# A chunked state-space scan on TensorE: held and moving operands exchanged, two heads in the column halves, outputs turned back and gated a step later

## Chip, cores and metric

One core of one Trainium2 chip runs the whole program, a two-block transformer stack in fp32, in one launch. The metric is the device time in microseconds (us) from start to end of an execution, as the median of several.

## What is computed

The first block holds a Mamba-2 branch beside differential attention; the rest (three feed-forward layers, projections, a second attention block) is not touched. The part that matters, cut down:

```python
SSD_HEADS, SSD_GROUPS, SSD_HEAD_DIM, SSD_STATE, SSD_CHUNK = 32, 4, 64, 128, 128     # 256 tokens: 2 chunks
X = x * dt                                        # (b, nc, Q, G, E, P), E = 8 heads of a group
a_cum = jnp.cumsum(dt * a_head, axis=-1)
Lmat = jnp.exp(jnp.where(causal, a_cum[..., :, None] - a_cum[..., None, :], -jnp.inf))
CB = jnp.einsum('bclgn,bcsgn->bgcls', Cc, Bc)
y_diag = jnp.einsum('bgcls,bgecls,bcsgep->bclgep', CB, Lmat, X)
states = jnp.einsum('bclgn,bgecl,bclgep->bcgepn', Bc, jnp.exp(a_cum[..., -1:] - a_cum), X)
y_off = jnp.einsum('bclgn,bcgepn,bgecl->bclgep', Cc, prev, jnp.exp(a_cum))
y = y_diag + y_off + d_skip * x
y = rmsnorm(group of (y * silu(z))) * norm_g      # groups of 512 channels
return y @ w_branch
```

## The kernel before

Every weight is cut into units of 1 MB that pass through a ring of five slots. SyncE loads a unit into RAW when TensorE has used the unit five before it (`w_used`); ScalarE rounds it to the high part WH (`split_hi`, L494); VectorE subtracts to get the low part WL (`split_lo`, L1092); TensorE then multiplies high by high, high by low and low by high (`parts`, L1803 to L1805). These two splits go on in every stage, one pair per unit.

There is no planner: each engine has its own block of code, executed in the order in which it is written, and the engines meet in named semaphores. The scan has eight blocks n = 2g + c (group g, chunk c) and nine steps r = 0 to 8. Step r prepares block r and multiplies block r-1, and between the steps stand one or two of the weight units of the q, k, v and gate projections (`beside(r)`: two in steps 2, 4, 6, 8).

- GpSimd (L1020 to L1044): `spread_cum(r + 1)` fetches the cumulated decay of the next block, spread over all partitions, into one of two DECAY buffers (L1029), after the products of block r-1 have been made (`ssd_y`). Then the skip term of block r goes to Y (L1042), which waits until block r-1 is normalised (`ys_ok`), as Y has one buffer.
- ScalarE (L777 to L801): eight Relu, one per head, and an Exp over 128x1024 turn the fetched rows into the decay matrices of block r (L784, L787). Then the state of a c = 0 block is copied (L792), and of the gated block r-1 the sum of squares and the reciprocal root are taken (L795, `rsqrt`). Then the weight splits and copies of the units beside.
- VectorE (L1410 to L1451): X dt of block r (L1418, which waits for `ssd_y`, as XDT has one buffer), for c = 0 also XDEC (L1420); block r-1: add the products from PS[3] (L1427), for c = 1 scale and add the part from the state (L1430, L1432), gate with silu(z) (L1434, signals `y_gated`); the masked CB (L1437), decay times CB (L1441, signals `ssd_m`); block r-1 normalised (L1444); the splits.
- TensorE (L2093 to L2129): CB of block r (L2099), for block r-1 the state product (L2111 or L2114) into PS[6], then eight products, one per head: the masked decay block 128x128 is held, XDT of 64 columns moves, and the output (tokens x 64) goes to PS[3] (L2117). fp32 operands make two passes each. Then the units beside.

```python
ins = mm(PS[3][:, e * SSD_P:(e + 1) * SSD_P], DECAY[n % 2][:, e, :], XDT[:, e * SSD_P:(e + 1) * SSD_P],
         start=True, stop=True)
```

In step 8 TensorE runs both gate units and turns the first normalised rows (`turn_rows`, L1987, into PS[7]); ScalarE and VectorE make high and low parts of them (L625, L1257), and the first gate sums are copied out (L761, `gate0_kept`). Then come the eight attention heads: scores (L2148, L2149), masked by VectorE (L1468), exponentials (L816), normalising (up to L1488, signals `attn_ok`), the transposes of the probabilities (L2141). Between them stand the units of ssd_w_branch, which multiply the turned scan outputs.

The rows of the second block's attention at L2306 (`pair_values`) also serve below: there two heads write to the two partition halves of PS[6], with a held operand 64 wide.

## Time and profile before

| | |
|---|---|
| median of 3 runs | 1108.06 us (1108.05 to 1108.44) |
| the profiled execution | 1108.8 us, span 1107.2 us |
| mean granted TensorE clock | 0.998 |
| TensorE busy | 1096.7 us, 99% of the span |
| VectorE busy | 770.8 us, 70% |
| ScalarE busy | 619.2 us, 56% |
| GpSimd busy | 36.5 us, 3% |
| DMA | 202.27 MB, mean 183 GB/s |

The span runs from the first to the last instruction of the profiled execution; the run's own time lies 1.6 us above it. Busy shares are means over the whole program. A busy TensorE need not be at its peak, since ends of matmuls are modelled; the start times are what tells a standstill. The scan occupies about 328 to 420 us.

### The profile page before, as it was taken

The numbers are of one execution on the slowest core, as the hardware profiler recorded it, in microseconds if no ns is written. First come the engines' busy times: TensorE is split into PE (matmuls) and PEld (weight loads), VectorE is DVE, ScalarE is ACT, GpSimd is POOL, SyncE is SP. The second block draws the span as 40 slices with busy tenths as digits, with TensorE's granted clock in tenths as the row PEclk, the third lists the DMA queues.
The fourth block names the chain that finished last, engine by engine and source line by source line (L and its number), as shares of the span: only waits on it lengthen the run. The fifth ranks groups of instructions, "written<-read, shape, count | busy, mean of one in ns | idle before, by whom it ended". The sixth has DMA issues, their size and how long they took to land.

```text
span 1107.2 us, 14788 instructions
## 1 busy us (share of the span) xinstructions
PE 1096.7 (99%) x6046; PEld 935.7 (85%) x6046; DVE 770.8 (70%) x897; ACT 619.2 (56%) x883; POOL 36.5 (3%) x66
## 2 busy tenths in 40 slices
PE   9999999999999999999999999999999999999997
PEld 7888888899999987778878888888978778888886
DVE  5866766687767778868768666675785667666664
ACT  7544445564577766655455454456776636444443
POOL 0000000000001100000000000000021100000000
PEclk9999999999999999999999999999999999999999
DMA  9656654755666545345566655645643445555551
GB/s 331 237 190 190 190 191 157 233 180 184 190 190 192 183 143 208 127 155 193 167 208 197 192 188 190 191 151 181 206 139 131 171 152 191 191 189 190 190 190 39
DMA packets 131667, 202.27 MB, mean 183 GB/s; under 512 B 5088, under 2 KB 98144, under 8 KB 131344
## 3 DMA queue, kind: packets, MB, share of 16 engines
q1 hardware_dynamic: 127920, 189.82, 52.7%
q0 software_dynamic: 2672, 10.65, 2.8%
q8 instruction: 48, 0.79, 0.3%
q10 hardware_dynamic: 1008, 0.86, 0.2%
q14 instruction: 19, 0.16, 0.0%
HBM read 200.24 MB, written 1.08 MB: 182 GB/s over the span
## 4 chain that ended last, share of the span: by engine, by line
PE 92%; DVE 3%; ACT 2%; issue 1%; DMA 1%; SPq 0%; DVEq 0%; ACTq 0%
PE TOP L1874 20%; PE ACC L1803 14%; PE ACC L1805 13%; PE ACC L1804 13%; PE TOP L1877 10%; PE TOP L1803 4%; PE TOP L1805 4%; PE TOP L1804 4%; ACT WH L494 1%; DVE WL L1092 1%; PE ACC L2117 1%; PE TOP L1719 1%; DMA H<-in_x 1%; PE TOP L2306 1%; PE TOP L2291 1%
## 5 line engine op out<-in xcount | busy, mean ns | idle before, releaser
L1092 DVE TENSOR_TENSOR WL<-RAW,WH 128x2048 fp32r<-128x2048 f32 (+3 forms) x177 | 400.1, 2264 | 114.0 <-ACT WH L494 113.7
L494 ACT ACTIVATE WH<-RAW 128x2048 fp32r<-128x2048 f32 (+1 forms) x179 | 337.6, 1890 | 68.7 <-DMA RAW<-in_ffn_w_gate 29.6
L1874 PE MATMUL TOP<-XT,WH 128*128 128x512 f32 x960 | 239.9, 392 | 0.0
L1874 PEld LDWEIGHTS TOP<-XT,WH 128*128 128x128 f32 x960 | 174.3, 189 | 32.4
L1803 PE MATMUL ACC<-WH,KTH 128*128 128x512 f32 (+1 forms) x452 | 178.6, 395 | 0.0
L1804 PE MATMUL ACC<-WL,KTH 128*128 128x512 f32 (+1 forms) x452 | 175.6, 389 | 0.0
L1805 PE MATMUL ACC<-WH,KTL 128*128 128x512 f32 (+1 forms) x452 | 175.6, 388 | 0.0
L1877 PEld LDWEIGHTS TOP<-XT,WL 128*128 128x128 f32 x960 | 131.0, 190 | 9.4
L1877 PE MATMUL TOP<-XT,WL 128*128 128x256 f32 x960 | 133.9, 282 | 0.0
L540 ACT ACTIVATE SCR<-TOP 128x512 f32<-128x512 f32 x60 | 35.8, 596 | 162.0 <-PE TOP L1877 162.0
L1805 PEld LDWEIGHTS ACC<-WH,KTL 128*128 128x128 f32 x452 | 84.8, 188 | 17.9
L1803 PEld LDWEIGHTS ACC<-WH,KTH 128*128 128x128 f32 x452 | 85.0, 188 | 17.1 <-DVE KTL L1259 0.7
L1804 PEld LDWEIGHTS ACC<-WL,KTH 128*128 128x128 f32 x452 | 85.1, 188 | 15.4
L1136 DVE TENSOR_TENSOR SCR<-TOP,SCR 128x512 f32<-128x512 f32 x60 | 41.4, 691 | 74.4 <-ACT SCR L540 74.4
L1803 PE MATMUL TOP<-WH,XT 128*128 128x512 f32 (+1 forms) x184 | 73.3, 398 | 0.4 <-DVE WL L1092 0.2
L1805 PE MATMUL TOP<-WH,XT 128*128 128x512 f32 (+1 forms) x184 | 71.2, 387 | 0.0
L1804 PE MATMUL TOP<-WL,XT 128*128 128x512 f32 (+1 forms) x184 | 71.1, 387 | 0.0
L1803 PE MATMUL ACC<-XT,WH 128*128 128x256 f32 x208 | 59.3, 285 | 0.0
L1804 PE MATMUL ACC<-XT,WH 128*128 128x256 f32 x208 | 58.8, 283 | 0.0
L1805 PE MATMUL ACC<-XT,WL 128*128 128x256 f32 x208 | 58.8, 283 | 0.0
L1803 PE MATMUL ACC<-WH,XT 128*128 128x512 f32 x144 | 58.4, 405 | 0.1
L1805 PE MATMUL ACC<-WH,XT 128*128 128x512 f32 x144 | 56.4, 391 | 0.0
(311 smaller groups left out, 1452.1 us busy)
## 6 DMA issues: line engine op xcount, KB each, us to landing
RAW<-in_w_in SPq DMA_DIRECT2D x50, 1024.0 KB, 5.2
RAW<-in_ffn_w_down SPq DMA_DIRECT2D x22, 1024.0 KB, 5.0
RAW<-in_ffn_w_gate SPq DMA_DIRECT2D x20, 1024.0 KB, 5.3
RAW<-in_ffn_w_up SPq DMA_DIRECT2D x20, 1024.0 KB, 5.4
RAW<-in_w_down SPq DMA_DIRECT2D x11, 1024.0 KB, 4.9
RAW<-in_w_gate SPq DMA_DIRECT2D x10, 1024.0 KB, 5.3
RAW<-in_w_up SPq DMA_DIRECT2D x10, 1024.0 KB, 5.3
RAW<-in_ssd_w_branch SPq DMA_DIRECT2D x8, 1024.0 KB, 5.0
```

The source lines that it names most:

```text
L494: nc.scalar.activation(WH[:, s, 0:n], RAW[:, s, 0:n], ACT.Copy).then_inc(w_hi, 1)
L540: nc.scalar.activation(LOW[n], TOP[:, bank:bank + 2, TOK:2 * TOK], ACT.Copy).then_inc(low_kept, 1)
L1092: tt(WL[:, s, 0:n], RAW[:, s, 0:n], WH[:, s, 0:n].bitcast(F32), ALU.subtract).then_inc(w_lo, 1)
L1136: tt(by_block(dst), TOP[:, bank:bank + 2, 0:TOK], LOW[n], ALU.add).then_inc((gate_sum, up_sum)[n], 1)
L1719: ins = nc.tensor.transpose(PS[6 + q][:, k * P:(k + 1) * P], XN[:, t, j * P:(j + 1) * P], IDENT)
L1803: mm(ps, stat_hi, mov_hi, start=first, stop=False)
L1804: mm(ps, stat_hi, mov_lo, start=False, stop=False)
L1805: return mm(ps, stat_lo, mov_hi, start=False, stop=last)
L1874: mm(PS[bank], WH[:, slot(c), ws], XT[:, k, :, :].rearrange("p u t -> p (u t)"), start=k == 0, stop=False)
L1877: ins = mm(PS[bank][:, TOK:2 * TOK], WL[:, slot(c), ws], XTH[:, k, :], start=False, stop=k == KD - 1)
L2117: ins = mm(PS[3][:, e * SSD_P:(e + 1) * SSD_P], DECAY[n % 2][:, e, :], XDT[:, e * SSD_P:(e + 1) * SSD_P], start=True, stop=True)
L2291: ins = nc.tensor.transpose(PS[5][:, b * P:(b + 1) * P], SC[q % 2][:, b * P:(b + 1) * P], IDENT)
```

## The change

The products of a block are made the other way round: XDT of a head (128 x 64) is held, the masked decay block of 128 columns moves, and the output is (64 channels x 128 tokens). Even heads go to partitions 0 to 63 of PS[7], odd heads to 64 to 127, so they use the two column halves of the array. The output is thus turned. ScalarE copies it to a free part of V or GAIN (`heads_turned`, signals `yt_kept`), and in the next step TensorE turns it back into PS[3] with four transposes (`turn_back`, signals `y_turned`). VectorE adds, gates and normalises block r-2 in step r (`gated`, `normed`), ScalarE takes its squares there (`squares`, with the discarded output in PS[3] instead of T1, as T1 now holds the scaled state part for a step, `off_ok`). The last block is turned back, gated and normalised among the gate units of step 8. Since PS[7] is taken, the second v unit moves to banks 4 and 5, and the first gate unit to banks 0 and 1, with their waits. GpSimd's code is the same.

```diff
--- before.py
+++ after.py
@@ -318,6 +318,7 @@
             sem, ("dt_abs", "dt_exp", "a_ok", "cums", "cums_exp", "cum_columns"))
         ssd_cb, ssd_cbm, ssd_e, ssd_m, xdec_ok, ssd_y, ssd_st = map(
             sem, ("ssd_cb", "ssd_cb_masked", "ssd_decay", "ssd_mix", "ssd_xdec", "ssd_y", "ssd_state"))
+        yt_kept, y_turned, off_ok = map(sem, ("y_turned_kept", "y_turned_back", "off_diagonal_scaled"))
         state_ok, skip_ok, y_read, y_gated, y_rms, ys_ok = map(
             sem, ("state_ok", "skip_ok", "y_read", "y_gated", "y_rms", "ys_ok"))
         k_turned, k_hi, k_lo = map(sem, ("k_turned", "k_hi", "k_lo"))
@@ -363,7 +364,7 @@
             return U_GATE + 2 * n - 2 if n else U_GATE0
 
         def gate_bank(n, t):
-            return ((4, 0), (4, 5), (6, 7), (4, 5))[n][t]
+            return ((0, 1), (4, 5), (6, 7), (4, 5))[n][t]
 
         def in2_bank(n, t):
             return ((4, 5), (0, 1), (4, 5))[n][t]
@@ -375,7 +376,11 @@
             return 5 - n % 2 if n else 0
 
         def v_bank(n, t):
-            return ((0, 1), (7, 5))[n][t]
+            return ((0, 1), (4, 5))[n][t]
+
+        def heads_turned(n):
+
+            return V[:, 0, 0:512] if n < 4 else GAIN[:, 0:512]
 
 
         def slot(c):
@@ -772,6 +777,12 @@
                         nc.scalar.activation(V[:, t, (n - 9) * 256:(n - 7) * 256], PS[v_bank(n // 2 - 4, t)][:],
                                              ACT.Copy).then_inc(qkv_kept, 1)
 
+            def squares(n):
+
+                act.wait_ge(y_gated, n + 1)
+                own.inc(nc.scalar.activation(PS[3][:], Y, ACT.Square, accum_out=SS[:, 4:5]))
+                rsqrt(RS[:, 4:5], SS[:, 4:5], n + 1, y_rms, 1.0 / GW)
+
             qkv(U_QKV)
             u = U_QKV + 1
             for r in range(9):
@@ -787,16 +798,17 @@
                     nc.scalar.activation(E, E, ACT.Exp, scale=-1.0).then_inc(ssd_e, 1)
                 if r:
                     n = r - 1
+                    act.wait_ge(ssd_y, r)
+                    nc.scalar.activation(heads_turned(n), PS[7][:], ACT.Copy).then_inc(yt_kept, 1)
                     if n % 2 == 0:
                         act.wait_ge(ssd_st, n + 1)
                         nc.scalar.activation(STATE, PS[6][:], ACT.Copy).then_inc(state_ok, 1)
-                    act.wait_ge(y_gated, n + 1)
-                    act.wait_ge(ssd_m, min(r + 1, 8)) if r < 8 else None
-                    own.inc(nc.scalar.activation(T1, Y, ACT.Square, accum_out=SS[:, 4:5]))
-                    rsqrt(RS[:, 4:5], SS[:, 4:5], n + 1, y_rms, 1.0 / GW)
+                if r >= 2:
+                    squares(r - 2)
                 for _u in range(beside(r)):
                     if u == U_GATE0 + 1:
                         kt_hi(0, 0)
+                        squares(7)
                     qkv(u)
                     u += 1
 
@@ -1406,6 +1418,22 @@
             def heads_bc(ap):
                 return ap.unsqueeze(2).to_broadcast([P, HPG, SSD_P])
 
+            def gated(n):
+
+                g, c = divmod(n, 2)
+                dve.wait_ge(skip_ok, n + 1)
+                dve.wait_ge(y_turned, n + 1)
+                own.link(tt(Y, PS[3][:], Y, ALU.add))
+                if c:
+                    own.link(tt(Y, Y, T1, ALU.add))
+                tt(Y, Y, BUF2[:, c, g * GW:(g + 1) * GW], ALU.mult).then_inc(y_gated, 1)
+
+            def normed(n):
+
+                g, c = divmod(n, 2)
+                dve.wait_ge(y_rms, n + 1)
+                stt(BUF2[:, c, g * GW:(g + 1) * GW], Y, RS[:, 4:5], GAIN[:, g * GW:(g + 1) * GW], ALU.mult, ALU.mult).then_inc(ys_ok, 1)
+
             split_lo()
             for r in range(9):
                 if r < 8:
@@ -1419,19 +1447,14 @@
                     if c == 0:
                         tt(by_head(XDEC), by_head(XDT), heads_bc(EX[:, 1, c, g * HPG:(g + 1) * HPG]),
                            ALU.mult).then_inc(xdec_ok, 1)
-                if r:
-                    n = r - 1
-                    g, c = divmod(n, 2)
-                    dve.wait_ge(skip_ok, r)
-                    dve.wait_ge(ssd_y, r)
-                    own.link(tt(Y, PS[3][:], Y, ALU.add))
-                    if c:
-                        dve.wait_ge(ssd_st, r)
-                        own.link(tt(by_head(T1), by_head(PS[6][:]),
-                                    heads_bc(EX[:, 0, c, g * HPG:(g + 1) * HPG]), ALU.mult))
-                        own.link(tt(Y, Y, T1, ALU.add))
-                    zs = BUF2[:, c, g * GW:(g + 1) * GW]
-                    tt(Y, Y, zs, ALU.mult).then_inc(y_gated, 1)
+                if r >= 2:
+                    gated(r - 2)
+                if r and r % 2 == 0:
+
+                    g, c = divmod(r - 1, 2)
+                    dve.wait_ge(ssd_st, r)
+                    tt(by_head(T1), by_head(PS[6][:]), heads_bc(EX[:, 0, c, g * HPG:(g + 1) * HPG]),
+                       ALU.mult).then_inc(off_ok, 1)
                 if r < 8:
                     dve.wait_ge(ssd_cb, r + 1)
                     tt(CBM[:], PS[2][:, 0:P], UPTO, ALU.mult).then_inc(ssd_cbm, 1)
@@ -1439,16 +1462,15 @@
                     dve.wait_ge(ssd_e, r + 1)
                     E = DECAY[r % 2]
                     tt(E, E, CBM[:].unsqueeze(1).to_broadcast([P, HPG, P]), ALU.mult).then_inc(ssd_m, 1)
-                if r:
-                    dve.wait_ge(y_rms, r)
-                    stt(zs, Y, RS[:, 4:5], GAIN[:, g0(n) * GW:(g0(n) + 1) * GW], ALU.mult, ALU.mult).then_inc(ys_ok, 1)
-                else:
-                    def g0(n):
-                        return n // 2
+                if r >= 2:
+                    normed(r - 2)
                 for _u in range(beside(r)):
                     if r == 8 and _u:
                         kt_lo(0)
+                        dve.wait_ge(off_ok, 4)
+                        gated(7)
                     split_lo()
+            normed(7)
 
 
             slopes = [2.0 ** (-8.0 * (h + 1) / DA_HEADS) for h in range(DA_HEADS)]
@@ -2082,9 +2104,18 @@
                     channels(u, q_bank(n))
                 elif n % 2 == 0:
                     v = n // 2 - 4
-                    first_half(u, (v_bank(v, 0), v_bank(v, 1)), lambda t: pe.wait_ge(qkv_kept, 7) if v else pe.wait_ge(conv_done, 12))
+                    first_half(u, (v_bank(v, 0), v_bank(v, 1)), lambda t: pe.wait_ge(qkv_kept, 7 + v) if v else pe.wait_ge(conv_done, 12))
                 else:
                     second_half(u, (v_bank(n // 2 - 4, 0), v_bank(n // 2 - 4, 1)))
+
+            def turn_back(n):
+
+                pe.wait_ge(yt_kept, n + 1)
+                if n:
+                    pe.wait_ge(y_rms, n)
+                for b in range(4):
+                    ins = nc.tensor.transpose(PS[3][:, b * P:(b + 1) * P], heads_turned(n)[:, b * P:(b + 1) * P], IDENT)
+                ins.then_inc(y_turned, 1)
 
             qkv(U_QKV)
             pe.wait_ge(conv_silu, 12)
@@ -2103,31 +2134,34 @@
                     g, c = divmod(n, 2)
 
                     if n:
-                        pe.wait_ge(y_gated, n)
+                        turn_back(n - 1)
                     pe.wait_ge(cums_exp, 1)
                     pe.wait_ge(cum_cols, 1)
                     if c == 0:
                         pe.wait_ge(xdec_ok, n // 2 + 1)
+                        if n:
+                            pe.wait_ge(off_ok, n // 2)
                         mm(PS[6][:], B0[:, g * P:(g + 1) * P], XDEC, start=True, stop=True).then_inc(ssd_st, 1)
                     else:
                         pe.wait_ge(state_ok, n // 2 + 1)
                         mm(PS[6][:], CT[:, g, P:TOK], STATE, start=True, stop=True).then_inc(ssd_st, 1)
                     pe.wait_ge(ssd_m, r)
+
                     for e in range(HPG):
-                        ins = mm(PS[3][:, e * SSD_P:(e + 1) * SSD_P], DECAY[n % 2][:, e, :], XDT[:, e * SSD_P:(e + 1) * SSD_P],
-                                 start=True, stop=True)
+                        ins = mm(PS[7][(e % 2) * SSD_P:(e % 2 + 1) * SSD_P, (e // 2) * P:(e // 2 + 1) * P],
+                                 XDT[:, e * SSD_P:(e + 1) * SSD_P], DECAY[n % 2][:, e, :], start=True, stop=True)
                     ins.then_inc(ssd_y, 1)
                 for _u in range(beside(r)):
                     if u < U_GATE0:
                         qkv(u)
                     elif u == U_GATE0:
-                        first_half(u, (4, 0), lambda t: pe.wait_ge(qkv_kept, 8 + t))
+                        first_half(u, (0, 1), lambda t: pe.wait_ge(qkv_kept, 9 + t))
                         pe.wait_ge(qkv_kept, 12)
+                        turn_back(7)
                         turn_rows(0, BUF2, 0)
                     else:
-                        second_half(u, (4, 0))
+                        second_half(u, (0, 1))
                     u += 1
-            pe.wait_ge(gate0_kept, 1)
             for h in range(9):
                 if h == 8:
                     pe.wait_ge(s_ready, 8)
```

How the order moves, at two places. TensorE, step 7 (block 6); TOP holds banks 4 to 7 and ACC banks 0 to 3. Before:

```order
L2099 MATMUL ACC<-XN 128x128 [waits ssd_cb_masked]
L2111 MATMUL TOP<-SCAN,SCR 128x512 [waits cum_columns,ssd_xdec,cums_exp,y_gated]
L2117 MATMUL ACC<-SCAN,SCR 128x64 [waits ssd_mix]
L2117 MATMUL ACC<-SCAN,SCR 128x64 x7
```

Now:

```order
L2130 MATMUL ACC<-XN 128x128 [waits ssd_cb_masked]
L2117 MATMUL ACC<-TAB,GAIN 128x128 [waits y_rms,y_turned_kept]
L2117 MATMUL ACC<-TAB,GAIN 128x128 x3
L2144 MATMUL TOP<-SCAN,SCR 128x512 [waits ssd_xdec,off_diagonal_scaled,cum_columns,cums_exp]
L2151 MATMUL TOP<-SCR,SCAN 64x128 [waits ssd_mix]
L2151 MATMUL TOP<-SCR,SCAN 64x128 x7
```

Four transposes stand ahead of the state product, and the moving operand has 128 columns.

VectorE from the first gating operation of step 8 to the first attention head. L1092 is a weight split, L1257 the low part of the turned rows. Before:

```order
L1427 TENSOR_TENSOR SCAN<-ACC,SCAN 128x512 [waits ssd_y,skip_ok]
L1430 TENSOR_TENSOR SCR<-TOP,EX 128x512 [waits ssd_state,dve_steps]
L1432 TENSOR_TENSOR SCAN<-SCAN,SCR 128x512 [waits dve_steps]
L1434 TENSOR_TENSOR SCAN<-SCAN,BUF 128x512 [waits dve_steps]
L1444 SCALAR_TENSOR_TENSOR BUF<-SCAN,RS,GAIN 128x512 [waits y_rms]
L1092 TENSOR_TENSOR WL<-RAW,WH 128x2048 [waits weights_hi]
L1257 TENSOR_TENSOR KTL<-TOP,KTH 128x512 [waits k_hi]
L1092 TENSOR_TENSOR WL<-RAW,WH 128x2048 [waits weights_hi]
L1468 SCALAR_TENSOR_TENSOR SCR<-TAB,TOP 128x384 [waits scores,ys_ok]
```

Now (L1104 is the split, L1269 the low part, L1426 to L1429 `gated`, L1435 `normed`, L1456 the scaled state part):

```order
L1426 TENSOR_TENSOR SCAN<-ACC,SCAN 128x512 [waits y_turned_back,skip_ok]
L1429 TENSOR_TENSOR SCAN<-SCAN,BUF 128x512 [waits dve_steps]
L1456 TENSOR_TENSOR SCR<-TOP,EX 128x512 [waits ssd_state]
L1435 SCALAR_TENSOR_TENSOR BUF<-SCAN,RS,GAIN 128x512 [waits y_rms]
L1104 TENSOR_TENSOR WL<-RAW,WH 128x2048 [waits weights_hi]
L1269 TENSOR_TENSOR KTL<-TOP,KTH 128x512 [waits k_hi]
L1426 TENSOR_TENSOR SCAN<-ACC,SCAN 128x512 [waits y_turned_back,skip_ok,off_diagonal_scaled]
L1428 TENSOR_TENSOR SCAN<-SCAN,SCR 128x512 [waits dve_steps]
L1429 TENSOR_TENSOR SCAN<-SCAN,BUF 128x512 [waits dve_steps]
L1104 TENSOR_TENSOR WL<-RAW,WH 128x2048 [waits weights_hi]
L1435 SCALAR_TENSOR_TENSOR BUF<-SCAN,RS,GAIN 128x512 [waits y_rms]
L1490 SCALAR_TENSOR_TENSOR SCR<-TAB,TOP 128x384 [waits scores,ys_ok]
```

The gating of block 7 (ending in L1429) now stands behind the low part L1269, and a weight split stands between it and its normalisation.

## Rows read from the trace of the kernel before

**Rows 1.** Waits of TensorE's matmuls, 318 to 430 us: total, times, longest
```profile
PE TOP L2141 <- DVE SCR L1488: 0.6, 1, 0.6
```
**Rows 2.** Timeline of TensorE: start us, duration us, engine, line, operation
```profile
426.45 0.39 PE L1805 MATMUL ACC<-WH,KTL 128*128 128x512 f32 x1
427.41 0.55 PE L2141 MATMUL TOP<-TAB,SCR 128*128 128x128 f32 x3 [0.57 <-DVE SCR L1488]
```
**Rows 3.** Chain of waits, 376 to 428 us: start us, us, what
```profile
376.44 1.74 PE ACC L2117 x16
378.21 0.70 DVE SCAN L1418
```
**Rows 4.** Timeline of TensorE, scan products of steps 2 and 4
```profile
338.92 1.89 PE L2117 MATMUL ACC<-SCAN,SCR 128*128 128x64 f32 x16
340.62 0.36 PE L1803 MATMUL TOP<-XT,WH 128*128 128x256 f32 x1
...
361.91 1.89 PE L2117 MATMUL ACC<-SCAN,SCR 128*128 128x64 f32 x16
```
**Rows 5.** Timeline of TensorE, two heads in column halves in the second block
```profile
865.17 0.39 PE L1805 MATMUL ACC<-WH,XT 128*128 128x512 f32 x1
865.49 0.43 PE L2306 MATMUL TOP<-BUF,V 128*64 128x256 f32 x1
...
865.97 0.27 PE L2306 MATMUL TOP<-BUF,V 128*64 128x128 f32 x1
865.98 0.27 PE L2306 MATMUL TOP<-GAIN,V 128*64 128x128 f32 x1
...
866.09 0.27 PE L2306 MATMUL TOP<-GAIN,V 128*64 128x128 f32 x1
866.29 0.44 PE L2291 MATMUL TOP<-TAB,BUF 128*128 128x128 f32 x2
```
**Rows 6.** Timeline of TensorE, four transposes between gate products
```profile
413.82 0.60 PE L1987 MATMUL TOP<-TAB,BUF 128*128 128x128 f32 x4
...
414.48 0.40 PE L1804 MATMUL TOP<-WL,XT 128*128 128x512 f32 x1
```
**Rows 7.** GpSimd: timeline, issues by size with median us to landing, all of L1029
```profile
386.82 0.58 POOL L1029 DMA_DIRECT2D SCR<-cum_rows  x1 [1.81 <-PE ACC L2117]
...
406.95 1.05 POOL L1042 TENSOR_TENSOR SCAN<-BUF,ROWS 128x512 f32<-128x512 f32 x1 [10.80 <-DVE BUF L1444]
...
SCR<-cum_rows POOLq DMA_DIRECT2D x6, 512.0 KB, 4.0
...
DMA to landing us min/median/max: 3.7/4.2/5.0
```
**Rows 8.** Timeline of ScalarE, step 7
```profile
398.85 2.44 ACT L784 ACTIVATE SCR<-SCR,DT 128x128 f32<-128x128 f32 x8
...
402.28 0.58 ACT L792 ACTIVATE SCAN<-TOP 128x512 f32<-128x512 f32 x1
404.89 0.63 ACT L795 ACTIVATE SCR<-SCAN 128x512 f32<-128x512 f32 x1 [2.03 <-DVE SCR L1441]
...
406.11 1.91 ACT L494 ACTIVATE WH<-RAW 128x2048 fp32r<-128x2048 f32 x1
```
**Rows 9.** Timeline of VectorE, steps 7 and 8 to the first head
```profile
401.92 0.69 DVE L1427 TENSOR_TENSOR SCAN<-ACC,SCAN 128x512 f32<-128x512 f32 x1
...
403.57 1.22 DVE L1441 TENSOR_TENSOR SCR<-SCR,CBM 128x1024 f32<-128x1024 f32 x1
406.12 0.75 DVE L1444 SCALAR_TENSOR_TENSOR BUF<-SCAN,RS,GAIN 128x512 f32<-128x512 f32 x1 [1.32 <-ACT RS L500]
408.06 2.29 DVE L1092 TENSOR_TENSOR WL<-RAW,WH 128x2048 fp32r<-128x2048 f32 x1 [1.19 <-ACT WH L494]
410.26 0.68 DVE L1427 TENSOR_TENSOR SCAN<-ACC,SCAN 128x512 f32<-128x512 f32 x1
...
421.34 1.01 DVE L1468 SCALAR_TENSOR_TENSOR SCR<-TAB,TOP 128x384 f32<-128x384 f32 x2
```

## The prediction

> **What bounds the kernel now.** The page first: a mean granted clock of 0.998 (2.4 GHz), and TensorE busy in 99% of the span, so the first question is whether the scan costs TensorE time. The list of waits over 318 to 430 us then says that TensorE is held there by another engine once, before the transposes of the first attention head, by VectorE [rows 1]. In order of time this is a gap of 0.96 us between two matmul starts [rows 2] where 0.23 is usual, so 0.73 us of real standstill. The reader is to see that this one gap decides what a saving in the scan is worth. The chain of waits says what leads to it: after the scan matmuls that start at 376.44 it leaves TensorE and stays with VectorE and ScalarE until 427.41 [rows 2, 3]. TensorE can gain whatever it likes between these times; the first head's transposes move only if the vector and scalar chain moves. Behind them TensorE is full again, so **the time of the kernel moves by as much as that start moves**.
>
> **TensorE's work.** I number scan steps by the loop index r; step r holds the products of block r-1. Old products: 16 passes (eight heads, two passes each), from first start to the next matmul 1.70 us [rows 4]. The new form (stationary operand 64 wide, 128 moving columns, two heads in the two column halves) exists in the second block's attention: both halves start 0.00 to 0.01 us apart, and the 128-column passes follow each other at 0.11 us [rows 5]. Four head pairs of two passes are 8 x 0.11 = 0.88 us. Entering costs 0.32 instead of 0.23 us (865.17 to 865.49), leaving 0.20 instead of 0.11 (866.09 to 866.29): 0.09 + 0.09. So 1.06 us, and 0.64 less per step, 5.1 for eight. The outputs now have to be turned back: four transposes per block. From 413.82 to 414.48 there are four of them and one 0.23 us matmul [rows 6]: 0.43 us, eight times 3.5 us. Net TensorE saves 0.21 us per step and 1.6 us before the first head.
>
> The row shows what a switch into and out of column halves costs, 0.18 us together. The Trainium skill, "TensorEngine Tiling (Array Packing)", Overview, promises up to 2x where a free dimension is at most 64, and says under Key Properties that changing the tiling mode drains the engine. By its 2x alone the eight steps would cost 6.8 instead of 13.6 us and TensorE would save 3.3 us in all; the trace agrees with the drain, and the sum goes by the rows.
>
> **The copy out on ScalarE** (PS[7] to V or GAIN) is one 128x512 copy per step as for STATE, 0.58 us of which some 0.1 overlaps what follows, so 0.48 [rows 8]; it lies before the squares. VectorE's operations are the same ones, moved. The squares now write to PS[3], for which no row stands: between 0.05 us less and 0.1 us more each; I take nothing. Moving v and gate banks adds no wait that I find, since the copies that free them are a unit old.
>
> **The queue that nothing was changed in: GpSimd.** Its order is: fetch decay block r+1, multiply the skip term of block r (which waits for the normalised block r-1, ys_ok), fetch block r+2, and so on. Before, the normalisation of block r-1 stood in step r, and the fetch waited for the scan matmuls alone (1.81 us idle before it) [rows 7]. Now block r-2 is normalised in step r, after that step's mask multiply, and the next fetch stands behind the skip multiply that waits for it. So a loop closes: fetch, ScalarE's eight Relu and Exp 3.43, copies 0.48 (0.96 in every second step), squares to reciprocal root 1.22 [rows 8], 0.83 from the start of the normalisation to that of the skip [rows 7, 9], skip 1.05, fetch 4.0 from issue to landing [rows 7]. That is 11.0 and 11.5 in turn, just over 11.2 us a step. Two steps take TensorE 22.99 us now (338.92 to 361.91 [rows 4]), less 2 x 0.21: 11.3 us each. The loop just fits, with almost nothing to spare.
>
> **The walk to the first head,** in the time of the profiled run. The scan of step 5 is released at 376.44 now [rows 3]; four steps have saved 0.21 each by then: 375.6, done 1.0 later. VectorE: X dt 0.7 [rows 3]; add, gate and CB mask 1.65, one more add for this block 0.72; decay multiply 1.23 [rows 9]: the normalisation of block 3 starts at 380.9. Skip 381.8, fetch 382.8, landed 386.8. ScalarE 3.43 + 0.48 + 1.22: 391.9. Skip, fetch, landed 0.83 + 1.05 + 4.0 later: 397.8. ScalarE with two copies: 403.4, block 5 normalised. Then the tail, where VectorE's and ScalarE's splits (2.20 and 1.91 us [rows 8, 9]) alternate with it: ScalarE split and VectorE split 407.5, gating of block 6 1.33, squares 1.22: 410.1 (block 6 is normalised at 406.12 now). Two splits again: 414.2. Low part of the turned rows 0.6 (a 128x512 operation that nothing waits for at once), gating of block 7 three times 0.72: 417.0. Squares: 418.2. ScalarE split 420.2, VectorE split 422.4, last normalisation: 423.2. The first head's scores are masked at 421.34 now [rows 9]. **The first head comes 1.8 us later**, although TensorE would be there 1.6 us earlier. What costs this: the gating of block 7, which starts at 410.26 [rows 9], now stands behind a weight split of each engine and the low part of the turned rows, and starts at 414.9; one weight split less follows it. TensorE will show two waits: up to 2 us for the copies of the first gate sums, which now stand behind these squares and a split on ScalarE (done at 420.2 + 1.0), and 2 to 3 us before the first head.
>
> The profiled run took 1108.8 us, the median of the runs shown is 1108.06, 0.7 below. Against the median: 1108.06 + 1.8 = **1109.9 us**. A measurement of this kernel can tell about 0.2%, 2.2 us, from no change; the forecast is on the slow side of none.
>
> **Rivals.**
> 1. *The fetch loop binds harder.* The median over the scan is 4.0 us; all eight fetches lie between 3.7 and 5.0 [rows 7], and they will now start at other moments of the weight loads. If they take 4.6, each of the four rounds from step 4 on adds 0.6 or nearly: 2.4 us, 1112.3; with another 0.3 us per round for GpSimd's order 1113.5. For: 11.2 against 11.3 leaves no slack. Against: the median of six in this very stretch is 4.0. It decides from a round above 11.3 us. Chance 0.22.
> 2. *The halves don't overlap here.* Passes of the two halves one after the other: 16 x 0.11 + 0.18 = 1.94 us, and TensorE loses 0.24 + 0.43 a step, 5.4 us, 1113 to 1116. Against: [rows 5] are the same form, source kind and bank sharing. Chance 0.05.
> 3. *TensorE leads the chain after all.* If the reorder takes the gating off VectorE's path and the fetches land in 3.7 us, the chain follows the earlier ends of the scan, and the 1.6 us are paid out: 1106.5. For: in the chain of before, ends of the scan release VectorE [rows 3]. Against: the gating of block 7 starts 4.6 us later, as walked. Chance 0.07.
> 4. *The halves are worth their full factor* and TensorE leads: 1108.06 - 3.3 = 1104.8, faster by 0.3%. In rows this is a block of 0.85 us with nothing to enter or leave, against the 0.18 measured. It is what the 2x of the page cited above would do. Chance 0.05.
>
> **How the numbers follow.** The forecast, 1108.6 to 1111.2 for its own terms (0.3 us per fetch either way over two to four rounds), has 0.61. Rival 1 reaches to 1113.5. The range from 1107.6 to 1113.3 leaves out rivals 3 and 4, nearly all of 2 and the end of 1. Slower by over 0.2% (above 1110.3) is rival 1, rival 2 and a quarter of the forecast, 0.42; faster by over 0.2% (under 1105.8) is rival 4, 0.05; the rest, 0.53, is within 0.2%.
>
> **What the changed profile would show.** The scan block of TensorE at about 1.06 us from first start to the next matmul, the halves starting together; four transposes in 0.43 us. ScalarE's first Relu of a step idle for the cum_rows transfer, up to 4 us in the steps after a short one (r = 4, 6) and about 1 us in r = 5 and 7. GpSimd's skip ahead of each fetch, which starts within 0.1 us of its end. VectorE's split of weights waiting some 3 us for ScalarE in the tail, TensorE waiting for gate0_kept and 2 to 3 us before the first head. Wrong would be: no wait of ScalarE for cum_rows (then the loop isn't there and the tail alone stands), a TensorE wait inside the scan (then the loop is slower than I walk it), or the first head's masked scores less than 46 us after the scan of step 5 starts (44.9 now, 47.6 as walked).

## The result, and the profile after

The changed kernel takes 1116.43 us (median of six runs, 1113.43 to 1118.12) against 1108.06 us for the kernel before (1107.94 to 1108.44): a ratio of 1.0072, 95% interval 1.0062 to 1.0082. It is slower by 8.4 us. The forecast was 1109.9 with a range to 1113.3, so the sign of its lean was right and its size was not. The profiled run of the change is the slowest of its six, 1.7 us above their median.

| | before | after |
|---|---|---|
| median of the runs, us | 1108.06 | 1116.43 |
| lowest to highest, us | 1107.94 to 1108.44 | 1113.43 to 1118.12 |
| profiled run: time, span, mean granted clock | 1108.8, 1107.2, 0.998 | 1118.12, 1116.1, 0.994 |
| first head's transposes start, us | 427.41 | 435.91 |

The first weight load of the stretch is issued at 323.08 us before and at 323.17 after, so the two traces can be laid side by side. The start of the first head's transposes moved by 8.5 us and the span by 8.9, so the bookkeeping of the prediction (the kernel's time moves by as much as that start) comes out to 0.4 us. Two things that it doesn't hold nearly cancel in this. Behind that start the granted clock of the change is 0.5 from 436.96 for 3.4 us, and the last weight load is issued at 1082.76 us against 1072.93, 9.8 us later. From there to the end of the span it is 33.4 us, against 34.3 before; why is not shown. The loss in the span arises between 323 and 441 us.

First what came as forecast. TensorE's timeline, step 5 (start us, duration us, engine, line, operation):

```profile
374.39 0.60 PE L2117 MATMUL ACC<-TAB,V 128*128 128x128 f32 x4
374.82 1.02 PE L2144 MATMUL TOP<-SCAN,SCR 128*128 128x512 f32 x2
375.78 1.09 PE L2151 MATMUL TOP<-SCR,SCAN 128*64 128x128 f32 x16
376.80 0.50 PE L1825 MATMUL ACC<-WH,XT 128*128 128x512 f32 x1
```

The turning back takes 0.43 us (374.39 to 374.82), and the sixteen passes 1.02 us (375.78 to 376.80) where they took 1.70 [rows 4]. So the two column halves do overlap. Now the waits, 318 to 440 us (engine, line, what it waited for: total us, times, longest):

```profile
POOL SCAN L1054 <- DVE BUF L1435: 76.4, 7, 13.2
...
ACT SCR L795 <- DMA SCR<-cum_rows: 16.8, 5, 6.1
...
DVE SCR L1464 <- ACT SCR L798: 8.3, 4, 4.5
...
PE ACC L2117 <- ACT RS L505: 3.5, 1, 3.5
```

ScalarE waits 16.8 us for the fetched decay blocks, VectorE's mask multiply 8.3 us behind it, and TensorE, inside the scan, once, 3.5 us, for a reciprocal root. GpSimd's timeline shows why. A DMA_DIRECT2D row is a fetch, TENSOR_TENSOR the skip multiply, and the brackets are the idle time before it:

```profile
345.48 1.03 POOL L1054 TENSOR_TENSOR SCAN<-BUF,ROWS 128x512 f32<-128x512 f32 x1 [13.19 <-DVE BUF L1435]
346.46 0.58 POOL L1041 DMA_DIRECT2D SCR<-cum_rows  x1
360.08 1.03 POOL L1054 TENSOR_TENSOR SCAN<-BUF,ROWS 128x512 f32<-128x512 f32 x1 [13.04 <-DVE BUF L1435]
361.07 0.59 POOL L1041 DMA_DIRECT2D SCR<-cum_rows  x1
...
374.84 0.58 POOL L1041 DMA_DIRECT2D SCR<-cum_rows  x1
...
388.25 0.59 POOL L1041 DMA_DIRECT2D SCR<-cum_rows  x1
...
399.27 0.57 POOL L1041 DMA_DIRECT2D SCR<-cum_rows  x1
```

Each fetch starts at the end of a skip multiply, as forecast. Most of them don't land as forecast. The view of the fetch lines over 318 to 440 us, and SyncE's timeline of the weight loads:

```profile
DMA to landing us min/median/max: 4.0/5.8/7.1
```
```profile
345.85 0.37 SPq L400 DMA_DIRECT2D RAW<-in_w_in  x1
360.10 0.37 SPq L400 DMA_DIRECT2D RAW<-in_w_in  x1
374.36 0.37 SPq L400 DMA_DIRECT2D RAW<-in_w_in  x1
```

The median of six was 4.0 before [rows 7] and is 5.8 now. The fetches at 346.46, 361.07 and 374.84 start 0.61, 0.97 and 0.48 us behind a weight load of 1 MB and take 7.1, 6.8 and 5.9 us. The one at 388.25, with no load within 5 us ahead of it, takes 4.0. Before, a fetch stood some 3.1 us behind its load (361.02 and 364.10). The DMA view of 345.8 to 349.9 us, by queue, tells what the fetch does in that time (packets, MB, share; q1 is SyncE's queue, q0 GpSimd's, and a queue without packets has no line):

```profile
q1 hardware_dynamic: 436, 0.89, 70.7%
```

In the 3.4 us after its issue the fetch has not one packet; the load has all 436. Some of this is there without a load too: the fetch issued at 388.25 has no packet before 389.5 either. But from 347.8 to 349.9 the load alone fills the 16 engines to 98.3% of their time (first line below), and only with the load's last packets do those of the fetch begin, 349.9 to 350.5 (the other two lines):

```profile
q1 hardware_dynamic: 381, 0.78, 98.3%
```
```profile
q1 hardware_dynamic: 90, 0.16, 67.8%
q0 software_dynamic: 28, 0.11, 46.4%
```

Both queues run on the same 16 engines (GpSimd's fills 100% of them from 390 to 391 us), and the fetch **waits until the weight load has nearly drained**, some 2 us more than it needs without a load. The distance alone doesn't fix the time: in experiment 8 a fetch stands 0.61 us behind its load as well and lands after 5.8 us, not 7.1.

What follows from the late fetch is a standstill of TensorE inside the scan. Timeline of ScalarE, then of TensorE:

```profile
380.80 2.45 ACT L795 ACTIVATE SCR<-SCR,DT 128x128 f32<-128x128 f32 x8 [3.11 <-DMA SCR<-cum_rows]
...
385.20 0.60 ACT L783 ACTIVATE ACC<-SCAN 128x512 f32<-128x512 f32 x1
```
```profile
382.56 0.49 PE L2130 MATMUL ACC<-XN 128*128 128x128 f32 x2
386.53 1.08 PE L2117 MATMUL ACC<-TAB,GAIN 128*128 128x128 f32 x4 [3.48 <-ACT RS L505]
```

The transposes of block 4 wait for the reciprocal root of block 3 (the bank PS[3]). Its squares stand on ScalarE's queue behind eight Relus that wait for a fetch. The products themselves could not have started before 385.7 in any case, since VectorE's mask multiply waits for the same Relus and ends there (384.44, 1.23 us long); the wait for the root puts the transposes and the state product behind this as well. What that share costs was not tested. And the 3.48 us aren't all that is lost. The table of stretches (core 0: us, PE busy, PEld, DVE, ACT, POOL, then PEclk, DMA share, GB/s):

```profile
383.00:386.00 3.00, 0.05 (x1) 0.00 (x0) 1.23 (x1) 2.94 (x7) 0.00 (x0) 0.96 0.73 217
386.00:389.00 3.00, 2.47 (x6) 1.25 (x6) 1.39 (x2) 2.27 (x3) 1.58 (x2) 0.50 0.36 138
389.00:392.00 3.00, 3.00 (x19) 2.33 (x19) 2.35 (x2) 0.00 (x0) 0.00 (x0) 0.50 0.55 175
392.00:395.00 3.00, 3.00 (x13) 2.38 (x13) 2.78 (x5) 2.67 (x9) 0.00 (x0) 0.90 0.00 0
```

TensorE stood still, and the granted clock then was 0.50 (1.2 GHz) from 385.8 to 392.6 us; products that start 0.23 us apart start 0.43 us apart there. Last the tail, VectorE and TensorE:

```profile
421.52 0.68 DVE L1426 TENSOR_TENSOR SCAN<-ACC,SCAN 128x512 f32<-128x512 f32 x1
...
426.86 2.29 DVE L1104 TENSOR_TENSOR WL<-RAW,WH 128x2048 fp32r<-128x2048 f32 x1 [3.21 <-ACT WH L499]
429.07 0.74 DVE L1435 SCALAR_TENSOR_TENSOR BUF<-SCAN,RS,GAIN 128x512 f32<-128x512 f32 x1
429.84 1.02 DVE L1490 SCALAR_TENSOR_TENSOR SCR<-TAB,TOP 128x384 f32<-128x384 f32 x2
```
```profile
435.91 0.55 PE L2175 MATMUL TOP<-TAB,SCR 128*128 128x128 f32 x3 [2.14 <-DVE SCR L1510]
```

The masks of the first head start at 429.84 (421.34 in [rows 9]), with VectorE's split waiting 3.21 us for ScalarE's and TensorE 2.14 us before the head, behind which the granted clock falls to 0.5 once more. The tail has the shape that was walked, 6.6 us later than walked.

### The profile page after: what moved, and what is told of

The parts are those of the page before. It is cut to its first block, busy times and chain, and to the rows that moved or that the text cites. A ratio compares the mean times of both kernels' runs of the same rounds, so it can differ in the third digit from the quotient of the medians.

```text
span 1116.1 us, 14853 instructions
## 1 busy us (share of the span) xinstructions
PE 1100.3 (99%) x6078; PEld 934.4 (84%) x6078; DVE 770.9 (69%) x897; ACT 623.5 (56%) x891; POOL 36.2 (3%) x66
## 4 chain that ended last, share of the span: by engine, by line
PE 87%; ACT 4%; DMA 4%; DVE 3%; issue 1%; POOL 0%; ACTq 0%; DVEq 0%
PE TOP L1896 20%; PE ACC L1825 13%; PE ACC L1827 13%; PE ACC L1826 13%; PE TOP L1899 10%; PE TOP L1825 3%; PE TOP L1827 3%; PE TOP L1826 3%; DMA SCR<-cum_rows 3%; ACT SCR L795 1%; ACT WH L499 1%; PE TOP L1741 1%; DMA RAW<-in_ffn_w_up 1%; PE TOP L2340 1%; PE TOP L2325 1%
## 5 line engine op out<-in xcount | busy, mean ns | idle before, releaser
L1104 DVE TENSOR_TENSOR WL<-RAW,WH 128x2048 fp32r<-128x2048 f32 (+3 forms) x177 | 400.3, 2266 | 114.6 <-ACT WH L499 114.3
L1825 PE MATMUL TOP<-WH,XT 128*128 128x512 f32 (+1 forms) x176 | 69.9, 397 | 1.2 <-DVE WL L1310 0.9
L1827 PE MATMUL TOP<-WH,XT 128*128 128x512 f32 (+1 forms) x176 | 68.1, 387 | 0.0
L1826 PE MATMUL TOP<-WL,XT 128*128 128x512 f32 (+1 forms) x176 | 68.0, 386 | 0.0
L1825 PE MATMUL ACC<-WH,XT 128*128 128x512 f32 x152 | 62.0, 408 | 0.1
L1827 PE MATMUL ACC<-WH,XT 128*128 128x512 f32 x152 | 59.7, 393 | 0.0
L1826 PE MATMUL ACC<-WL,XT 128*128 128x512 f32 x152 | 59.5, 391 | 0.0
L1825 PE MATMUL ACC<-XT,WH 128*128 128x256 f32 x208 | 59.3, 285 | 0.0
```

The lines of the kernel that those rows point to most:

```text
L1104: tt(WL[:, s, 0:n], RAW[:, s, 0:n], WH[:, s, 0:n].bitcast(F32), ALU.subtract).then_inc(w_lo, 1)
L1825: mm(ps, stat_hi, mov_hi, start=first, stop=False)
L1826: mm(ps, stat_hi, mov_lo, start=False, stop=False)
L1827: return mm(ps, stat_lo, mov_hi, start=False, stop=last)
```

## The experiments

Lines of experiments are those of their own kernels, shifted by one to three from the change's. Each batch had runs of the kernel before beside it: medians of 1108.15 (first four), 1108.08 (next three) and 1108.47 (last three).

**1. The fetch ahead of the skip.** The change, with GpSimd's queue reordered:

```diff
                 if r == 0:
                     spread_cum(0)
-                if r < 7:
-                    spread_cum(r + 1)
+                    spread_cum(1)
+                if r < 6:
+                    spread_cum(r + 2)
```

> The changed kernel, with GpSimd's fetch of decay block r+2 put ahead of skip(r) instead of behind it, so that it waits for scan product r alone. Theory A (queue order): the 8.4 us come from the fetch, which now stands behind a normalisation one step late, starts within 1 us of a 1 MB weight load and lands after 5.6 to 7.1 us instead of 4; each step then waits for it, ScalarE blocks the squares, TensorE stalls 3.75 us and its clock falls to 1.2 GHz. Then here the landings are 4.0 to 4.7 us, the 3.75 us gap and the half clock near 386 us are gone, and the time is 1107.5 to 1110 us. Theory B (the turn-back path itself, products to copy to transposes to gating, costs): no more than 2 us come back, 1114 us or more. Theory C (the new tail ahead of the first attention head costs): the stalls in the scan go, but 1110 to 1113 us stay.

1109.78 us (1108.72 to 1111.04), ratio 1.0015 (1.0006 to 1.0025). In its profile, GpSimd's timeline and the view of the fetch lines, 353 to 385 us:

```profile
353.69 0.57 POOL L1041 DMA_DIRECT2D SCR<-cum_rows  x1 [7.92 <-PE TOP L2152]
...
384.66 0.58 POOL L1041 DMA_DIRECT2D SCR<-cum_rows  x1 [2.37 <-PE TOP L2152]
```
```profile
DMA to landing us min/median/max: 3.8/4.1/4.8
```

The fetch is released by the scan products again, ScalarE waits for none, and TensorE has no gap over 0.9 us before 419 us. (Over 318 to 440 us the six landings lie between 3.8 and 5.4 us; the 5.4 is the first one, 5.6 in the change.) The mean clock is 1.000 in the profiled run and 0.997 to 1.000 in all ten. 6.7 of the 8.4 us are back: theory A. What is left is 1.6 us; the time is within A's range and 0.2 us short of C's. These 1.6 us lie in the tail (experiment 5).

**2. The queue order alone, in the kernel before.** No halves, no turning back, gating unmoved:

```diff
                 if r == 0:
                     spread_cum(0)
-                if r < 7:
-                    spread_cum(r + 1)
+                    spread_cum(1)
...
                                         skip.unsqueeze(2).to_broadcast([P, HPG, SSD_P]), ALU.mult).then_inc(skip_ok, 1)
+                if 1 <= r < 7:
+                    spread_cum(r + 1)
```

> The kernel before, with one edit: GpSimd's fetch of decay block k is queued behind skip(k-1), so that it waits for the normalisation of block k-2 in the step before its use, the same wait that the changed kernel has; no column halves, nothing turned back, gating not moved. Theory A (queue order): this alone costs most of the loss, 1112 to 1118 us, with landings above 5 us where the fetch starts within 1.5 us of a weight load, and 4 us elsewhere. Theory B (the turn-back path costs): close to the kernel before, 1108 to 1109.5 us.

1116.83 us (1116.17 to 1118.07), ratio 1.0077 (1.0060 to 1.0094). A kernel that computes exactly as before is as slow as the change once its fetch stands behind a late normalisation. Theory A, but not the same loop: the fetches follow each other at 12.1 to 14.2 us (353.02, 367.19, 379.26, 392.48), and each round here also holds the mask multiply of 1.22 us, since ScalarE's squares wait for it in the kernel before. Their landings have a median of 4.9 us. The fetches at 367.19 and 392.48, with no load within 6 us ahead, land after 4.0 and 4.1 us, and their rounds are still 12.1 us: here part of the loss is the loop by itself. TensorE stood 1.79 and 1.87 us in two steps, and behind the second the granted clock was 0.5 for 6.8 us, so this one edit brings the clock's part of the loss, too.

**3. Collisions taken away, the loop kept.** The change, with SyncE holding five weight loads:

```diff
                 if c >= RING:
                     sp.wait_ge(w_used, c - RING + 1)
+                k = {8: 3, 10: 4, 11: 5, 13: 6, 15: 7}.get(c - U_QKV)
+                if k:
+                    sp.wait_ge(cum_spread[k % 2], 16 * (k // 2 + 1))
```

> The changed kernel, queue order of GpSimd kept, but SP holds the weight loads that coincide with a fetch (five of them) until that fetch has landed. Theory A1 (the loop fits, as forecast, as long as the fetch lands in 4 us; the weight load ahead of it in the DMA engines is what breaks it): landings 4.0 to 4.6 us, no stall above 1 us in the scan, 1109 to 1111 us. Theory A2 (the loop over GpSimd binds by itself, contention adds little): landings as short, but ScalarE still waits over 1 us per step for them and the time stays 1112 us or more.

1110.85 us (1109.39 to 1112.17), ratio 1.0023 (1.0013 to 1.0034). GpSimd's timeline, and the view of the fetch lines:

```profile
359.42 0.59 POOL L1044 DMA_DIRECT2D SCR<-cum_rows  x1
...
370.93 0.58 POOL L1044 DMA_DIRECT2D SCR<-cum_rows  x1
...
382.37 0.59 POOL L1044 DMA_DIRECT2D SCR<-cum_rows  x1
...
393.03 0.58 POOL L1044 DMA_DIRECT2D SCR<-cum_rows  x1
```
```profile
DMA to landing us min/median/max: 3.7/4.1/5.4
```

With the fetch landing in 4.1 us the rounds are 11.5, 11.4 and 10.7 us, where 11.2 was worked out, and the kernel runs within 1 us of the forecast. (The round before these, from 345.62 to 359.42, takes 13.8 us here as well.) ScalarE still waits for four of the fetches, 9.6 us in all, and VectorE's mask multiply 4.5 us behind it, which was put down as a sign of A2; but TensorE doesn't wait in the scan, and the time is A1's: the loop is as forecast, the landing in the change isn't.

**4. Column halves undone, fetch ahead.** On top of experiment 1, blocks in whole rows into two banks in turn, which the gating and the squares use directly; no copy and no turning back:

```diff
                     for e in range(HPG):
-                        ins = mm(PS[7][(e % 2) * SSD_P:(e % 2 + 1) * SSD_P, (e // 2) * P:(e // 2 + 1) * P],
-                                 XDT[:, e * SSD_P:(e + 1) * SSD_P], DECAY[n % 2][:, e, :], start=True, stop=True)
+                        ins = mm(PS[3 if n % 2 else 7][:, e * SSD_P:(e + 1) * SSD_P], DECAY[n % 2][:, e, :],
+                                 XDT[:, e * SSD_P:(e + 1) * SSD_P], start=True, stop=True)
```

> The changed kernel with the fetch ahead of the skip, and the column halves undone: decay blocks held and inputs moving as before, products straight into one of two banks in turn (no copy to SBUF, no transposes), gating still one step later. The halves save 0.64 us of products and cost 0.43 us of transposes per step, 1.6 us before the first head; so 1 to 2 us more than e1_fetch_ahead if TensorE leads there, no difference (within 0.5 us) if the tail behind the last block sets the start of the first head, and less than e1_fetch_ahead if the copy and the transposes lie on the path to the last gating.

1111.39 us (1110.80 to 1112.72), ratio 1.0033 (1.0019 to 1.0046): 1.6 us more than experiment 1, as eight steps of 0.21 us would give. The copy and the transposes aren't on the path. The expectation tied such a loss to TensorE leading, and it does not lead here: it waits 2.13 us before the first head (2.14 in experiment 1). The tail sets that start in both kernels, but by the traces the tail itself hangs on the products of the scan (VectorE waits 9.4 us for them over the stretch in experiment 1), which come later by those 0.21 us a step.

**5. The last block's squares and normalisation moved out of the tail.** On top of experiment 1:

```diff
                     if u == U_GATE0 + 1:
                         kt_hi(0, 0)
-                        squares(7)
                     qkv(u)
                     u += 1
+            squares(7)
...
                     split_lo()
-            normed(7)
...
-            dve.wait_ge(ys_ok, 8)
+            dve.wait_ge(ys_ok, 7)
...
                     if h:
                         split_lo()
+                    else:
+                        normed(7)
```

(The squares of block 7 also write to T1 there, since PS[3] is taken by then.)

> e1_fetch_ahead with the last block's squares moved on ScalarE behind the two copies of the first gate, and its normalisation on VectorE behind the first head's maxima (into the time in which ScalarE takes the exponentials). Theory (the tail sets the rest): in e1_fetch_ahead the first head's scores are there at 418.8 us and are masked at 422.1, because the weight split waits for the squares (1.2 us) and the normalisation stands before the masks (0.75 us); with both out of the way the masks start near 419 us and the transposes of the first head 2.5 to 3.3 us earlier than in e1_fetch_ahead, so 1106 to 1107.5 us, faster than the kernel before. Rival (TensorE takes over: 424.6 us is as early as it can be at the first head's transposes, or the waits move into the second head): under 1 us of gain, 1109 us or more.

1105.79 us (1105.54 to 1106.63), ratio 0.9976 (0.9967 to 0.9985): 4.0 us under experiment 1, a little more than was expected, and **faster than the kernel before**, by 0.2%. In the profiled runs the first head's transposes start 3.5 us earlier (424.72 for 428.20); four of the ten runs of experiment 1 had a mean clock of 0.997 and took 1110.0 to 1111.0 us, where its profiled one had 1.000 and 1109.0, which may be the rest. VectorE's tail in experiment 1, then in this one, and this one's first head on TensorE:

```profile
415.25 0.69 DVE L1430 TENSOR_TENSOR SCAN<-SCAN,BUF 128x512 f32<-128x512 f32 x1
419.15 2.29 DVE L1105 TENSOR_TENSOR WL<-RAW,WH 128x2048 fp32r<-128x2048 f32 x1 [3.20 <-ACT WH L499]
421.36 0.74 DVE L1436 SCALAR_TENSOR_TENSOR BUF<-SCAN,RS,GAIN 128x512 f32<-128x512 f32 x1
422.13 1.02 DVE L1491 SCALAR_TENSOR_TENSOR SCR<-TAB,TOP 128x384 f32<-128x384 f32 x2
```
```profile
414.90 0.69 DVE L1430 TENSOR_TENSOR SCAN<-SCAN,BUF 128x512 f32<-128x512 f32 x1
415.51 2.28 DVE L1105 TENSOR_TENSOR WL<-RAW,WH 128x2048 fp32r<-128x2048 f32 x1
418.66 1.02 DVE L1490 SCALAR_TENSOR_TENSOR SCR<-TAB,TOP 128x384 f32<-128x384 f32 x2 [0.86 <-PE TOP L2185]
```
```profile
424.20 0.39 PE L1829 MATMUL ACC<-WH,KTL 128*128 128x512 f32 x1
424.72 0.55 PE L2177 MATMUL TOP<-TAB,SCR 128*128 128x128 f32 x3
```

The weight split follows the gating at once, the masks wait for TensorE's scores and for nothing else, and TensorE reaches the first head without the gap.

**6. The same tail in the kernel before.** The same two moves.

> The kernel before, with the same two moves of the last block's squares and normalisation. TensorE finishes the second half of the gate unit at 419.85 us there and the masks start at 421.34, so at most 1 us can be had: 1107 to 1108.1 us. If e5_tail_later gains over e1_fetch_ahead and this one hardly over the kernel before, the changed kernel's TensorE time is worth something only with its tail shortened.

1108.15 us (1107.33 to 1108.42), ratio 0.9999 (0.9990 to 1.0008): nothing. The moves alone are worth nothing to the kernel before; the gain of experiment 5 needs the rest of the change (experiment 10 tells how much of it is the halves').

**7. The deferral undone, halves kept.** The gating, squares and normalisation of block r-1 back in step r, and

```diff
                     ins.then_inc(ssd_y, 1)
+                    turn_back(n)
```

> The changed kernel with the column halves kept and the deferral undone: each block is copied, turned back and gated in its own step, TensorE waiting for ScalarE's copy right behind the products (GpSimd's order as in the change, its skip waiting for the block before as in the kernel before). Per step TensorE then waits for the end of the products, the copy (0.6 us) and what ScalarE is busy with (a weight split of 1.9 us in some steps), 1 to 2.5 us in eight steps: 1114 to 1126 us. If it were within 1 us of the kernel before, the deferral would not be needed.

1130.26 us (1126.32 to 1130.68), ratio 1.0190 (1.0175 to 1.0205), above the upper end. TensorE's timeline:

```profile
342.77 1.09 PE L2145 MATMUL TOP<-SCR,SCAN 128*64 128x128 f32 x16
346.35 0.66 PE L2113 MATMUL ACC<-TAB,V 128*128 128x128 f32 x4 [2.48 <-ACT V L802]
```

From the start of the last product to that of the first transpose it is 2.75 to 4.03 us in five steps and 0.97 in three, and the granted clock was at 0.5 three times, for 3.4 us each. The expectation had the copy behind a weight split; what it stands behind is longer, the Relus and the Exp of the next block (in this step 342.29 to 345.71). GpSimd's fetches are released by the scan products here, as before, so none of this is the queue order. The deferral is what makes the turning back free; its price is the queue order.

**8. The tail alone in the change** (fetch still behind the skip, the edit of experiment 5).

> The changed kernel with GpSimd's queue order kept (fetch behind the skip) and only the last block's squares and normalisation moved as in e5_tail_later. If the late fetches are the main loss and the tail a separate one of 1.5 to 4 us, this lies 4 us or more above e5_tail_later: 1110 to 1114 us, with the landings of 5 to 7 us and the TensorE gap behind the fourth or fifth fetch still there. If the tail were the main loss: under 1108 us.

1111.91 us (1109.67 to 1113.63), ratio 1.0028 (1.0016 to 1.0039), with a standstill of TensorE of 3.55 us up to 385.93 and landings up to 7.5 us.

**9. Loads held, with the tail** (experiments 3 and 5 together).

> e3_loads_held (queue order kept, five weight loads held until the fetch beside them has landed) with the same tail. Theory A1 (the loop over GpSimd fits as long as a fetch lands in 4 us): within 1 us of e5_tail_later, 1105.5 to 1107 us. Theory A2 (the loop binds by itself, and the tail hid it in e3_loads_held): 1108 us or more.

1106.69 us (1106.31 to 1108.68), ratio 0.9986 (0.9977 to 0.9995): 0.9 us above experiment 5, the intervals of the two overlapping. The loop over GpSimd, left as it is but without collisions, costs about that or less.

**10. Whole rows, with the tail** (experiments 4 and 5 together).

> e4_whole_rows_fetch_ahead (no column halves, no turning back, gating one step later) with the same tail. TensorE now sets the start of the first head, so the halves' net 0.21 us in eight steps shows: 1.5 to 2.2 us above e5_tail_later, 1107.3 to 1108.2 us. If the halves saved nothing, 1106 us.

1107.38 us (1106.88 to 1108.21), ratio 0.9988 (0.9979 to 0.9997): 1.6 us above experiment 5, or 1.2 if each is taken against the runs of the kernel before in its own batch. The halves are worth 1.2 to 1.6 us in eight steps. The kernel without them is 1.1 us faster than the kernel before beside it, but its trace doesn't show this in the scan: from the first weight load of the stretch to the last it takes 749.5 us (322.77 to 1072.31), the kernel before 749.9 (323.08 to 1072.93). What the deferral is worth by itself stays open.

## Why the prediction was right and wrong

- **TensorE's work**: right. 1.02 us a block for the forecast 1.06, 0.43 for the transposes; experiment 4 finds 1.6 us for all eight, as worked out, and experiment 10 1.2 to 1.6. Rivals 2 and 4 are out by the rows of step 5.
- **The loop over GpSimd**: right as a mechanism and in all its terms but one. The step that failed is the mis-sized term "fetch 4.0 from issue to landing". It was taken from fetches that all start 3.1 to 3.4 us behind a weight load; in the new order three of the six start 0.5 to 1.0 us behind one and take 5.9 to 7.1 us. Rival 1 named exactly this and priced it at 4.6 us, because the rows of before reach only to 5.0. With 6 to 7 us for it, a round is 13 to 14.5 us against 11.3: the fetches are 14.6, 13.8 and 13.4 us apart (the first of these proves little, as experiment 3 has 13.8 there without a collision). The fetch walked at 382.8 starts at 388.25, 5.5 us late, and the one after it lands after 5.0 us, 1.0 us more. With 0.1 us in the tail these are the 6.6 us by which the masks are later than walked. Experiment 3 puts the term back to 4.1 us and gets the forecast: its first load stands 0.75 us earlier than that of before, and with that added the fetch walked at 382.8 starts at 383.1 and the masks walked at 423.2 at 423.4.
- **A TensorE wait inside the scan** was named as what would prove the walk wrong. It came, 3.48 us between 382.6 and 386.5, and behind it a stretch at 1.2 GHz that no term of the sum held. The transposes' wait for the root of the block before was in the diff; I counted ScalarE's Relus as waiting and did not follow what is queued behind them.
- **The tail**: right. From the normalisation of block 5 (409.93) to the masks (429.84) it takes 19.9 us, walked 19.8. Experiment 1 has it without the loop: 1.6 us on the kernel's time. That the forecast of 1.8 lies so close is partly luck, as it was made for loop and tail together.
- **The bookkeeping**: right to 0.4 us, and partly by luck. 8.5 us on the first head's start, 9.8 on the last weight load (the clock fell behind that start), 8.9 on the span.
- **Rival 3** (TensorE leads) is what experiment 5 makes true, with 2.3 us under the kernel before. From the first weight load of the stretch to the last its trace takes 748.1 us (322.06 to 1070.18) for 749.9: 1.7 us of the 2.3, near the 1.6 that TensorE saves. The rest lies outside that stretch.

In sum, by medians: of 8.4 us, 5.6 go with the collisions of fetch and load, with the standstill and the half clock that they bring (the change less experiment 3); 1.1 with the loop itself (experiment 3 less 1, intervals that overlap); 1.6 are the tail. How the 5.6 divide between late fetches and the clock was not separated, but the clock is hardly most of it: the two runs of the change with the highest mean clocks, 0.998 and 0.997, took 1115.93 and 1113.43 us, the three with 0.994 1116.94 to 1118.12. The six runs of the change spread over 4.7 us, the six of before over 0.5. In the three later batches, with 18 to 22 runs, those of before spread over 1.8, 3.8 and 2.2 us, so that the change makes the time less certain is likely, but not shown.

## What to carry to other kernels

When an edit delays one operation, walk every queue for what stands behind the instruction that waits for it, here a fetch that needed nothing of it, and put what is free to go ahead of what waits. A transfer's time from issue to landing belongs to its moment as much as to its size: where the moment moves towards another engine's load, price it as queued behind nearly the whole load. And look at what the saved time runs into; here the saving showed only when two operations that nothing needed yet were taken out of the tail.

## What the runs showed of the hardware

- **A transfer on GpSimd's queue just behind a big one on SyncE's waits for nearly all of it.** GpSimd's 512 KB fetch, issued 0.61 us behind SyncE's 1 MB load, had no packet for 3.4 us and landed after 7.1; issued with no load ahead it had none for 1.3 us and took 4.0. The Trainium skill, "DMA: Bandwidth & Descriptors", Queues, rings and completion order, says that a DMA engine goes round robin between the queues that have work, packet by packet. Taken by the profile's packets, nothing of the kind shows between these two queues: 436 of the one, none of the other. This doesn't refute the page. By its figures a packet is 9 to 17 descriptors as a rule and 64 at most, while the profile's packets are 2 KB each here (0.89 MB in 436), which for a load of 1 MB makes, as an estimate, 32 on each of the 16 engines; they may be the page's descriptors. Whether the engine or the making of GpSimd's descriptors holds it back was not tried.
- **The clock falls after a standstill, not always.** After TensorE stood 3.48 us in the change the granted clock was 0.5 for 6.8 us, after 1.87 us in experiment 2 also for 6.8, and after 3.55 us in experiment 8 for 3.4. After some 2.1 us before the first head it was 0.5 for 3.4 us in the change and in experiment 3, and stayed 1.0 at the same place in experiments 1 and 4.
